# Merge's first gates behind the last recurrent unit, its first up-projection ahead of the last pooling group

## The reference, cut to what matters

```python
z = h @ w_in
u_pool, u_lru, g_pool, g_lru = split(z)
y_pool, new_pool = pool_mix(pool_buf, u_pool, ...)   # means over 2/4/8/16 rows minus the row, then a map per group
xc = causal_dwconv(lru_buf, u_lru, ...)
y_lru, new_h = rglru(lru_h, xc, ...)                 # h = a * h + u along the rows
merged = sigmoid(g_pool) * (y_pool @ w_pool_up) + sigmoid(g_lru) * (y_lru @ w_lru_up)
x = x + gate1 * rmsnorm(merged @ w_out, g_post1)
```

## Time and profile before

| | |
|---|---|
| median of 3 runs | 2338.44 us (2338.01 to 2340.0) |
| profiled execution | 2340.07 us |
| its slowest core, span | core 3, 2338.0 us |
| spans of the odd cores 1, 3, 5, 7 | 2330.4, 2338.0, 2337.3, 2334.4 us |
| spans of the even cores | 2307.7 to 2309.9 us |
| TensorE busy on the profiled page | 2094.1 us, 90% of the span |
| mean granted TensorE clock | 0.962 to 0.970 |

### The profile page before, as it was taken

One profiled execution on the slowest core, in us unless ns is written; L12 is line 12 of the kernel. 1 busy time (PEld: TensorE's weight loads), 2 busy tenths in 40 slices (PEclk: granted clock), 3 DMA queues, 4 the chain that ended last, 5 costly groups with the idle time before them and its releaser, 6 DMA issues.

```text
span 2337.3 us, 37485 instructions; the slowest of 8 cores (2307.7 to 2338.0 us)
## 1 busy us (share of the span) xinstructions
PE 2094.1 (90%) x14624; PEld 1025.7 (44%) x14624; DVE 1027.5 (44%) x2122; ACT 894.8 (38%) x1232; POOL 146.5 (6%) x281
## 2 busy tenths in 40 slices
PE   0348989897999999999899999999999898999995
PEld 0124444443445545555445555555554343444442
DVE  0346889997521111111246666642001676665003
ACT  1357877886310000002365455441103334443111
POOL 0000000000000000000000000000000000000000
PEclk9969999998999999999999999999999999999998
DMA  7996565555355676568899987768787997889983
GB/s 173 257 199 114 93 104 103 108 96 116 69 113 101 110 126 108 106 110 160 183 196 184 183 147 142 134 125 179 133 133 129 200 205 145 149 151 182 220 163 101
DMA packets 64743, 336.06 MB, mean 144 GB/s; under 512 B 7216, under 2 KB 7728, under 8 KB 32048
## 3 DMA queue, kind: packets, MB, share of 16 engines
q0 software_dynamic: 39888, 273.17, 67.0%
q1 hardware_dynamic: 24672, 60.40, 7.9%
HBM read 585.58 MB, written 21.12 MB: 260 GB/s over the span
## 4 chain that ended last, share of the span: by engine, by line
PE 79%; DMA 7%; ACT 7%; DVE 4%; issue 2%; another core or an unknown queue 1%; SPq 0%; DVEq 0%; ACTq 0%; POOLq 0%
PE ps_all L264 79%; ACT sb_R L241 5%; DMA sb_R<-x1s 4%; DVE sb_R L244 3%; DMA sb_R<-xp 2%; ACT L241 1%; DVE sb_R L247 1%; DMA sb_w<-w_in 0%; SPq L279 0%; ACT sb_rstd L241 0%; DVE sb_mod L254 0%; DVE sb_stl L247 0%; DVE sb_R L258 0%; SPq L287 0%
## 5 line engine op out<-in xcount | busy, mean ns | idle before, releaser
L264 PE MATMUL ps_all<-sb_R,sb_w 128*128 128x512 bf16 (+2 forms) x12288 | 1926.4, 319 | 34.8 <-ACT sb_R L241 33.1
L264 PEld LDWEIGHTS ps_all<-sb_R,sb_w 128*128 128x128 bf16 x12288 | 927.5, 98 | 1014.5 <-issue 61.1
L241 ACT ACTIVATE sb_R<-ps_all 128x128 f32<-128x128 f32 (+6 forms) x416 | 206.9, 531 | 626.9 <-PE ps_all L264 464.5
L247 DVE SCALAR_TENSOR_TENSOR sb_R<-sb_R,sb_cvec 128x384 f32<-128x384 f32 (+3 forms) x576 | 369.6, 689 | 30.4 <-ACT sb_R L241 19.6
L244 DVE TENSOR_TENSOR sb_R<-sb_R 128x579 bf16<-128x579 f32 (+9 forms) x148 | 160.5, 1084 | 179.1 <-ACT sb_R L241 125.6
L241 ACT ACTIVATE sb_R<-sb_R 128x512 f32<-128x512 f32 (+9 forms) x216 | 203.3, 963 | 92.1 <-DMA sb_R<-xp 57.1
L241 ACT ACTIVATE sb_wsm<-ps_all 128x579 bf16<-128x579 f32 (+1 forms) x64 | 40.0, 625 | 398.2 <-PE ps_all L264 398.2
L241 ACT ACTIVATE sb_R<-ps_all,sb_cvec 128x579 f32<-128x579 f32 (+4 forms) x184 | 166.3, 905 | 18.8 <-DVE sb_R L244 12.9
L264 PE MATMUL ps_all<-sb_R,sb_ones 128*128 128x512 bf16 (+1 forms) x144 | 43.3, 413 | 119.3 <-ACT sb_R L241 119.3
L244 DVE TENSOR_TENSOR sb_R<-sb_R,sb_mod 128x128 f32<-128x128 f32 x96 | 27.0, 291 | 267.4 <-ACT sb_R L241 263.7
L244 DVE TENSOR_TENSOR sb_R<-sb_R,sb_rstd 128x579 f32<-128x579 f32 (+5 forms) x128 | 116.3, 934 | 22.4 <-ACT sb_rstd L241 22.4
(11 more groups left out here) (48 smaller groups left out, 707.3 us busy)
## 6 DMA issues: line engine op xcount, KB each, us to landing
sb_w<-w_ffn_up POOLq DMA_DIRECT2D x96, 1024.0 KB, 10.9
sb_w<-w_ada POOLq DMA_DIRECT2D x48, 1024.0 KB, 13.4
sb_w<-w_ffn_down POOLq DMA_DIRECT2D x48, 1024.0 KB, 10.1
sb_w<-w_in POOLq DMA_DIRECT2D x36, 1024.0 KB, 10.0
sb_w<-w_out POOLq DMA_DIRECT2D x16, 1024.0 KB, 10.8
sb_R<-xm SPq DMA_DIRECT2D x4, 2182.0 KB, 62.2
sb_R<-xp SPq DMA_DIRECT2D x4, 2170.0 KB, 51.1
sb_w<-w_lru_up POOLq DMA_DIRECT2D x8, 1024.0 KB, 12.2
```

The costliest lines, as they stand in the source:

```text
L241: return self.P.op("act", lambda e: e.activation(out=out, in_=in_, func=func, **kw), after)
L247: return self.P.op("dve", lambda e: e.scalar_tensor_tensor(out=out, in0=in0, scalar=scalar, in1=in1, op0=op0, op1=op1), after)
L264: return self.P.op("pe", lambda e: e.matmul(out, lhsT=lhsT, rhs=rhs, start=start, stop=stop), after, signal)
```

## The change

1. In `lru`, `merge_first` is called in the last but one turn of the loop, behind `P1` of the last unit and `P3` of the unit before it. It now waits for what frees slot 0 instead of for the whole recurrent stage. The order behind it is `P2` and `P3` of the last unit.
2. In `rest`, the weight block of `Z(1)` is asked for ahead of `wgrp`, and `wgrp` is asked for there, behind `Z(2)`, no longer at the end of `lru`.
3. In `rest`, `merge_first` no longer stands between `W(1)` and `G(1)`. Merge's first up-projection from `y_lru` now stands there in part: its block and matmuls behind `G(1)`, then `W(0)`, then its two VectorE operations, then `G(0)`.
4. `merge` skips that up-projection for q = 0. Its jobs are split off into `up_jobs` and `gated_up`.

```diff
             P3(i)
+            if i == NU - 2:
+                self.merge_first(info[i]["fin"])
...
-        self.t_wgrp = self.ld(wgrp, self.w_grp, "wgrp", after=self.wsm_rel, eng="pool")
...
         def rest():
             Z(2)
+            w1 = self.wload(self.w_in, 1)
+            self.t_wgrp = self.ld(self.wgrp, self.w_grp, "wgrp", after=self.wsm_rel, eng="pool")
             E2(3, ev3)
             dt3 = W(3, ev3)
             ev2 = E(2)
             E2(2, ev2)
-            Z(1)
+            Z(1, w1)
...
             dt1 = W(1, ev1)
-            self.merge_first()
             G(1, dt1)
+            jobs = self.up_jobs(0, self.w_lup, 16, self.y_lru, self.t_ylru)
             dt0 = W(0, ev0)
+            self.gated_up(jobs, 2, self.merge_gates)
             G(0, dt0)
...
-        self.merge_gates = self.gates(20, 2, [self.t_lru])
+        self.merge_gates = self.gates(20, 2, slot0)
+
+    def up_jobs(self, q, wten, kch, opnd, t_op):
+        wsl, wt, wi = self.wload(wten, q, kch)
+        jobs = []
+        for j in range(2):
+            b = self.merge_ring.next()
+            tok = self.job(b, 3, [(0, 512), (512, 1024), (1024, N)],
+                           [(wsl[:, k, j * 128:(j + 1) * 128], (lambda c0, c1, k=k: opnd[:, k, c0:c1]),
+                             [wt, t_op[k * len(t_op) // kch]]) for k in range(kch)])
+            if j == 1:
+                self.w_rel[wi] = tok
+            jobs.append((b, tok))
+        return jobs
+
+    def gated_up(self, jobs, bi, tg):
+        for j, (b, tok) in enumerate(jobs):
+            g = self.gb[bi + j][:, 0:N]
+            tg[bi + j] = self.Vstt(g, g, 1.0, self.ap_ps(b, N), ALU.add, ALU.mult, [tok, tg[bi + j]])
+            self.release(b, 3, [tg[bi + j]])
...
+                if q or bi == 0:
+                    self.gated_up(self.up_jobs(q, wten, kch, opnd, t_op), bi, tg)
```

More of the change, by code:

```diff
@@ L889, in pool_first, with Z @@
         PR = 15 + NPR
-        def Z(g):
-            wsl, wt, wi = self.wload(self.w_in, g)
+        def Z(g, loaded=None):
+            wsl, wt, wi = loaded or self.wload(self.w_in, g)
             jobs = []
@@ L1009, in pool_first, with merge_first @@
         self.pool_rest = rest
-    def merge_first(self):
+    def merge_first(self, slot0):
         self.gb = [self.f32(O_GB, SN), self.f32(O_GB + 4 * SN, SN), self.rstd[:], self.f32(O_GB3, SN)]
         self.merge_ring = Ring([0, 3])
-        self.merge_gates = self.gates(20, 2, [self.t_lru])
+        self.merge_gates = self.gates(20, 2, slot0)
[16 more added lines that the diff above has]
+            self.release(b, 3, [tg[bi + j]])
     def gates(self, blk, bi, free):
@@ L1035, in merge @@
         y_pool, y_lru = self.y_pool, self.y_lru
-        gb, ring = self.gb, self.merge_ring
+        gb = self.gb
         merged = self.bfv(O_MERGED, 16, SNB)
         self.merged = merged
-        groups = [(0, 512), (512, 1024), (1024, N)]
         self.t_merged = []
```

## The result

The changed kernel takes 0.9946 of the time before, 95% interval 0.9930 to 0.9963: of 2338.44 us that is 2325.8, where 2325.0 was forecast. (In several executions of either kernel the cores of a die ran at a lower granted clock and took longer; the ratios leave these out, the medians over all executions, such as the changed kernel's 2426.99 us, do not.) The profiled execution took 2326.86 us. Its slowest core is core 5.

What follows compares the result with a forecast made beforehand. The odd cores set the time, with two TensorE waits of 12.52 and 4.86 us and slow clock behind each. Gaining 14.5 us and losing 1.1 takes 13.4 us off 2338.44, to 2325.0 us, range 2320 to 2332.

Steps and rivals of the forecast that it cites:

- The first hole: TensorE stands 12.52 us behind the last unit's map awaiting Z(2)'s weight block; gates fill it, gaining 14.5 us.
- The second hole: Ahead of G(0), 4.86 us waiting for VectorE's operand; moves ahead of G(1) as 6.5 us, costing 1.1 us.
- The sum: Up to the second ada item: 14.5 us from the first hole less 1.1 at the second, 13.4 us.
- the late stage: Between 1800 and 1940 us, up stage of half B, where TensorE waits when re-reads of x1 are late.
- What was costed at nothing behind that: After the second ada item both kernels run the same instructions in the same order; SP's queue keeps its order; no cost.
- rival 1: Gates' block lands late at the first hole, loads unserved until near 553.7 us; 9.8 us lost, 2334.8 us; 3 in 100.
- rival 2: Gates' load still leaves POOL at 557.9 us; 14.5 us not won, 1.1 lost, about 2339 us; 2 in 100.
- Rivals 3 and 4: Late-stage waits: three more, 2345.4 us, 3 in 100; one more, 2331.8, 8 in 100; one fewer, 2318.2, 5 in 100.

Runs made afterwards that it cites:

- the split version: Changed kernel with the first up-projection cut in two, one job ahead of G(1), one ahead of G(0): 0.9912 of the kernel before, 2318.05 to 2322.71 us.

## Why the prediction was right

**The first hole.** Its cause was read rightly and is shown twice: putting the wait for the map back ahead of the block brings the hole back (1.0004), and taking it away without moving the gates leaves half of the gain, with the new wait where the prediction's own list of ScalarE's order puts it. On three cores the 14.79 us of the gates went in at next to no price. Z(1) starts 32.9 us after the second pair of map jobs on cores 1, 3 and 7, where it did so after 32.4 to 33.7 before (588.16 - 555.26 = 32.9 on core 3); the bank wait is 0.35 instead of the 0.55 taken. On core 5 the clock fell behind the 1.82 us wait in the last map, and the same distance is 587.69 - 553.61 = 34.1 (31.8 before): 1.2 us that were not in the sum. The prediction had asked for 2.4 GHz from 558 us on as a sign of being right; there it did not hold.

**Edit 2 as a whole** was costed at nothing apart from the earlier blocks, which is right and shown: what counts is that the gates' block goes out ahead of wgrp, and the order of wgrp and the later blocks is free here, with some 3 us of cover.

**The second hole.** The wait was put at 6.5 us and is 6.52 on all four odd cores. That it is VectorE's chain W(1) the rows show (it ends at 629.75 + 1.37 = 631.12, G(1) starts at 631.37), and the split version agrees: it covers the chain with 7.4 us of independent matmuls and loses the wait. The slow clock behind it was taken from G(0) before, some 1.6 us over the 2.57 + 14.79 of G(1) and two jobs. Measured behind the same wait, G(1) and the up-projection took 3.60 + 15.73 us on core 5 but 3.39 + 14.80 on core 3, about 2 and 1 us over; cores 1 and 7 lie between, at 1.6 and 1.5. Core 3's rows, to be set beside those of core 5:

```profile
631.64 3.44 PE L264 MATMUL ps_all<-sb_R,sb_wsm 128*128 128x512 bf16 x12 [6.52 <-DVE sb_R L247]
635.03 14.96 PE L264 MATMUL ps_all<-sb_R,sb_w 128*128 128x512 bf16 x96
```

(The 2.57 us hold a bank wait of 0.40 that G(1) no longer has, so the slow clock itself cost some 0.4 us more, in the prediction's row of G(0) and here.)

**The sum.** Core by core the distance shrank by 14.5 us on core 3, 14.3 on core 7, 13.3 on core 1 and 10.9 on core 5, in the mean 13.2 where 13.4 were worked out. That the slowest core's span of 2324.1 us lies 0.5 from the 2324.6 of the sum is partly luck: it is another core, its distance is 1.2 us over the 114.1 worked out, and the late stage below cost it 2.3 us less than it had cost core 3.

**What was costed at nothing behind that** held, with a cover that got thinner. The tanh of merge's first pool gates waits until the pooled rows are stored:

```profile
667.48 1.08 ACT L241 ACTIVATE sb_R<-ps_all 128x1091 f32<-128x1091 f32 x1 [12.72 <-DMA o_pool_s<-sb_R]
```

That store took 10.5 to 11.7 us to land on the four odd cores (11.7 on core 5) where it had taken 8.5 to 8.8 before. Two weight blocks are asked for in that stretch on core 5 now, one was before on core 3; that these slow it was not tried. The tanh ended at 667.48 + 1.08 = 668.56, and TensorE wanted its banks at 669.75, 1.2 us later. The prediction said that SP's queue keeps its order, but did not look at how long this store on it takes to land.

**The rivals.** The late block (rival 1) and the unmoved block (rival 2) did not come; the second was built as an experiment and came out at its price. Rivals 3 and 4 did not either, on balance: TensorE's standing still from 1800 to 2000 us is 13.9 to 16.3 us on the four odd cores, where core 3 had 17.0 and core 1 10.8 before, the other two 16.9 and 15.3. The cores changed places, core 1 lost 5 us of its gain there, and the slowest core, now core 5, stood still 2.3 us less than core 3 had before (14.7 against 17.0). The run without re-reads shows that they are what is waited for. Which core gets the long ones in which execution stays open; in the changed kernel's second measurement core 3 ended at 2310.6 us and core 7 at 2323.8, from one program.

## What to carry to other kernels

When a load lands late, look at what stood at the head of its queue while the transfer engines were idle: here one load that had to wait for a matmul held four that did not the earlier trace rows. Asking earlier pays only as far as the engine then finds work whose operands and banks are free, so a block and the work that it feeds have to move together. A job that covers one wait can leave another; here two short chains were better covered by two jobs of their own length than by one long one on either side.

## What the runs showed of the hardware that was not expected

The cost of a wait in clock is not a fixed price. Behind the same wait of 6.52 us in the same program, the up-projection's two jobs, 14.79 us at a granted clock of 1.00, took 14.80 us on core 3, 15.22 and 15.35 on cores 7 and 1, and 15.73 on core 5. Behind the wait of 1.82 us in the last unit's map cores 1, 3 and 7 kept 2.4 GHz (2.15 us for 12 matmuls), and core 5 did not (2.83 us; granted clock 0.77 in the mean from 556 to 561 us):

```profile
556.00:561.00 5.00, 5.00 (x27) 2.21 (x26) 1.07 (x1) 4.22 (x4) 1.05 (x2) 0.77 0.96 275
```

In the two profiles of the split version, where no long wait stands behind it, the distance is 106.3 us on six of eight odd cores, and 107.4 on the two whose last map was slow (2.80 and 2.81 us): the fall costs 1.1 us there.
